# Norms in two halves of tokens, with the low parts made for two chunks at once

## The reference

```
# first block, per layer
h = layer_norm(ALPHA * h + 0.5 * swiglu(h, up1, down1), g0, b0)
h = layer_norm(ALPHA * h + mixer(h), g1, b1)          # mixer ends with  merged @ w_o
h = layer_norm(ALPHA * h + 0.5 * swiglu(h, up2, down2), g2, b2)
# behind it the 16 learned tokens are dropped; second block, per layer
x = x + token_mixing(rmsnorm(x, g_mix), ...)          # ends with  merged @ w_out
x = x + swiglu_2(rmsnorm(x, g_ffn), ...)              # layer 0: dense
x = x + moe_swiglu(rmsnorm(x, g_ffn), ...)            # layer 1: router, 8 experts, top 2
return rmsnorm(x, g_final)

layer_norm(x, g, b) = (x - mean(x)) * rsqrt(mean((x - mean(x))**2) + 1e-5) * g + b
rmsnorm(x, g)       = x * rsqrt(mean(x*x) + 1e-6) * g
```

## Time and profile before

| | us |
|---|---|
| three runs | 2657.14, 2655.45, 2654.16 |
| median | 2655.45 |
| span of the profiled execution | 2653.2 |
| PE busy | 2561.1 (97%) |
| DVE busy | 1943.4 (73%) |
| ACT busy | 1614.8 (61%) |
| POOL busy | 377.1 (14%) |

### The profile page before, as it was taken

One profiled execution on the slowest core, in us unless ns is written; L12 is line 12 of the kernel. 1 busy time (PEld: TensorE's weight loads), 2 busy tenths in 40 slices (PEclk: granted clock), 3 DMA queues, 4 the chain that ended last, 5 costly groups with the idle time before them and its releaser, 6 DMA issues.

```text
span 2653.2 us, 65470 instructions
## 1 busy us (share of the span) xinstructions
PE 2561.1 (97%) x27736; PEld 2159.7 (81%) x27736; DVE 1943.4 (73%) x1886; ACT 1614.8 (61%) x1690; POOL 377.1 (14%) x440
## 2 busy tenths in 40 slices
PE   9999999999999999999999999999999999999998
PEld 8887788888887888897888888799778687787775
DVE  5467675564567765666765466689999999999997
ACT  4346653354357654455654446657888888887876
POOL 3211322121105221103021103031000000000000
PEclk9999999999999999999999999999999999999999
DMA  8574355555555655554455655378999999999996
GB/s 268 172 210 141 108 195 197 169 190 188 157 161 152 199 182 181 177 192 132 148 197 192 190 190 163 118 273 340 412 419 422 419 413 422 413 418 418 413 421 273
DMA packets 345255, 666.16 MB, mean 251 GB/s; under 512 B 20448, under 2 KB 273536, under 8 KB 306096
## 3 DMA queue, kind: packets, MB, share of 16 engines
q1 hardware_dynamic: 344192, 661.39, 69.0%
q0 software_dynamic: 528, 0.63, 0.3%
q10 hardware_dynamic: 288, 0.59, 0.1%
HBM read 661.49 MB, written 1.05 MB: 250 GB/s over the span
## 4 chain that ended last, share of the span: by engine, by line
PE 62%; DVE 19%; DMA 7%; ACT 6%; issue 4%; DVEq 2%; POOLq 0%; ACTq 0%; POOL 0%; SPq 0%
PE ps L2336 17%; PE ps L2338 17%; PE ps L2337 17%; DVE w_lo L1621 7%; DMA w<-in_moe_units 3%; DVE work L1621 2%; DMA mix<-in_moe_units 2%; DVE ff L1621 2%; DVE w_lo L1461 2%; ACT w_hi L958 2%; ACT w_hi L849 2%; DMA squares_and_low<-in_moe_units 1%; PE ps L2379 1%; PE ps L2385 1%; PE ps L2380 1%
## 5 line engine op out<-in xcount | busy, mean ns | idle before, releaser
L2336 PE MATMUL ps<-x_hi,w_hi 128*128 128x96 f16 (+2 forms) x5024 | 1076.1, 246 | 19.1 <-DVE w_lo L1621 5.8
L2338 PE MATMUL ps<-x_hi,w_lo 128*128 128x96 f16 (+2 forms) x5024 | 1075.4, 246 | 7.3 <-issue 7.3
L2337 PE MATMUL ps<-squares_and_low,w_hi 128*128 128x96 f16 (+2 forms) x5024 | 1075.5, 246 | 4.3 <-issue 4.3
L1461 DVE SCALAR_TENSOR_TENSOR w_lo<-w,w_hi 128x2048 f16<-128x2048 f32 (+4 forms) x335 | 680.8, 2043 | 295.0 <-ACT w_hi L849 293.2
L849 ACT ACTIVATE w_hi<-w 128x2048 f16<-128x2048 f32 (+4 forms) x335 | 556.8, 1671 | 85.7 <-PE ps L2338 74.8
L2336 PEld LDWEIGHTS ps<-x_hi,w_hi 128*128 128x128 f16 x5024 | 492.6, 98 | 76.0 <-issue 15.9
L2337 PEld LDWEIGHTS ps<-squares_and_low,w_hi 128*128 128x128 f16 x5024 | 492.6, 98 | 50.0 <-issue 5.3
L2338 PEld LDWEIGHTS ps<-x_hi,w_lo 128*128 128x128 f16 x5024 | 492.4, 98 | 49.1 <-issue 7.4
L2338 PE MATMUL ps<-ff,w_lo 128*128 128x272 f16 (+1 forms) x880 | 243.3, 276 | 0.0
L2337 PE MATMUL ps<-ff,w_hi 128*128 128x272 f16 (+1 forms) x880 | 243.3, 276 | 0.0
L2336 PE MATMUL ps<-ff,w_hi 128*128 128x272 f16 (+1 forms) x880 | 243.3, 276 | 0.0
(11 more groups left out here) (408 smaller groups left out, 4770.9 us busy)
## 6 DMA issues: line engine op xcount, KB each, us to landing
w<-in_ffn_w_up_units SPq DMA_DIRECT2D x176, 512.0 KB, 4.6
w<-in_moe_units SPq DMA_DIRECT2D x75, 1024.0 KB, 11.9
w<-in_moe_units SPq DMA_DIRECT2D x56, 1280.0 KB, 15.3
mix<-in_moe_units SPq DMA_DIRECT2D x50, 1024.0 KB, 12.0
w<-in_w_in SPq DMA_DIRECT2D x96, 512.0 KB, 4.8
mix<-in_moe_units SPq DMA_DIRECT2D x36, 1280.0 KB, 15.6
w<-in_mix_w_in SPq DMA_DIRECT2D x60, 512.0 KB, 5.0
squares_and_low<-in_moe_units SPq DMA_DIRECT2D x26, 1024.0 KB, 12.0
```

Of the source, the lines that this page charges most:

```text
L1461: vec.scalar_tensor_tensor(k.w_lo[:, s, 0:size], k.w32[:, s, 0:size], WS, k.w_hi[:, s, 0:size], ALU.mult, ALU.subtract).then_inc(k.parts_r ...
L2336: pe.matmul(acc, w_hi, x_hi, start=first, stop=False)
L2337: pe.matmul(acc, w_hi, x_lo, start=False, stop=False)
L2338: return pe.matmul(acc, w_lo, x_hi, start=False, stop=last)
```

## The change

Each of the eight seams goes in two halves of tokens (2 x 136 or 2 x 128). The last two units of down, and the last of wo and of layer 0's wout, are gone through twice, once for each half, into two banks of their own; three tiles into the second half PE makes the sums of the first. DVE, ACT and the sums work half by half, and the opening of the next product takes all eight chunks of the first half, with the sums of the second half behind its fourth chunk, and then the second half. Low parts are used two chunks behind the high ones. The 13 fillers of a norm go.

On DVE, centring, scaling by the reciprocal and the low parts take two chunks in one instruction. Weight and bias columns are no longer in these: a new tensor_scalar with two columns writes the residual `h` for each chunk and half, from which the low part is taken. ACT makes the high part of each chunk and half with both columns (scale and bias), and no longer writes the residual. The splits of the next product's third unit move: DVE's from ahead of the last addition to behind the norm (or, behind wo, into the next product's own program), ACT's to between the second root and the second half's high parts. The second layer's router norm keeps its form.

The diff, cut to the programs' core (`th` is a half of the tokens, PAIRS is 4):

```diff
-KEEP_WARM = 13
...
+END_BANKS, MEAN_BANKS, VAR_BANKS, RMS_BANKS = (6, 7), (4, 7), (5, 6), (5, 4)
+OPEN_TOGETHER, LAG, SUMS_AT = 5, 2, 3
...
-    for u in range(phase.units):
+    for u in range(phase.units - 1):
...
+        def high(p, pair):
+            th = part_of(t, p)
+            act.wait_ge(k.ln_scaled, 2 * PAIRS * n + PAIRS * p + pair + 1)
+            for c in (2 * pair, 2 * pair + 1):
+                if last:
+                    act.activation(k.sq2[:, c, part_of(ALL2, p)], k.sq[:, c, th], ACT.Square, bias=column(k, b0 + c),
+                                   scale=column(k, g0 + c)).then_inc(k.rms_squared, 1)
+                else:
+                    act.activation(k.x_hi[:, c, th], k.sq[:, c, th], ACT.Identity, bias=column(k, b0 + c),
+                                   scale=column(k, g0 + c)).then_inc(k.x_hi_ready, 1)
...
+        squares_of_end(0)
+        rest_square(0)
+        root(0)
+        high(0, 0)
+        high(0, 1)
+        squares_of_end(1)
+        high(0, 2)
+        rest_square(1)
+        high(0, 3)
+        root(1)
         if following is not None:
             split(following + 2, q, UNIT)
...
+        def over_pair(x):
+            return x.unsqueeze(1).broadcast_to([P, 2, (t.stop - t.start) // 2])
+        def centered(p, pair):
+            th = part_of(t, p)
+            x = k.h[:, 2 * pair:2 * pair + 2, th]
+            vec.tensor_tensor(x, x, over_pair(k.ps[:, MEAN_BANKS[p], th]), ALU.subtract)
+        def inverse(p):
+            th = part_of(t, p)
+            vec.wait_ge(k.ln_std, 2 * n + p + 1)
+            vec.reciprocal(k.rstd[:, 0, th], k.std[:, 0, th])
+            vec.drain()
+        def normed(p, pair):
+            th, c = part_of(t, p), slice(2 * pair, 2 * pair + 2)
+            vec.tensor_tensor(k.sq[:, c, th], k.h[:, c, th], over_pair(k.rstd[:, 0, th]), ALU.mult).then_inc(k.ln_scaled, 1)
+            if pair + 1 < PAIRS:
+                centered(p, pair + 1)
+            vec.drain()
+            for c in (2 * pair, 2 * pair + 1):
+                vec.tensor_scalar(k.h[:, c, th], k.sq[:, c, th], column(k, g0 + c), column(k, b0 + c), ALU.mult, ALU.add)
+        def low(p, pair):
+            if n < LN_PARTS:
+                th, c = part_of(t, p), slice(2 * pair, 2 * pair + 2)
+                vec.wait_ge(k.x_hi_ready, high_before(n, False) + KC * p + 2 * pair + 2)
+                vec.tensor_tensor(k.x_lo[:, c, th], k.h[:, c, th], k.x_hi[:, c, th], ALU.subtract).then_inc(k.x_ready, 1)
         vec.drain()
-        def t(c):
-            vec.scalar_tensor_tensor(k.sq[:, c, cols], k.h[:, c, cols], column(k, g0 + c), k.rstd[:, 0, cols],
-                                     ALU.mult, ALU.mult).then_inc(k.ln_scaled, 1)
-            if c + 1 < KC:
-                u(c + 1)
-        def lo(c):
-            return vec.scalar_tensor_tensor(k.x_lo[:, c, cols], k.sq[:, c, cols], column(k, b0 + c), k.x_hi[:, c, cols], ALU.add, ALU.subtract)
-        def plain(c):
-            vec.tensor_scalar(k.h[:, c, META:T1], k.sq[:, c, META:T1], column(k, b0 + c), None, ALU.add)
-        for c in range(KC + 1):
-            if last:
-                if c < KC:
-                    t(c)
-                if c > 0:
-                    plain(c - 1)
-            else:
-                scaled(c, t, lo, (n + 1) * KC)
-            vec.drain()
+        add_end(0)
+        vec.drain()
+        spread(0)
+        centered(0, 0)
+        inverse(0)
+        normed(0, 0)
+        normed(0, 1)
+        low(0, 0)
+        add_end(1)
+        normed(0, 2)
+        low(0, 1)
+        spread(1)
+        normed(0, 3)
+        low(0, 2)
+        centered(1, 0)
+        inverse(1)
+        low(0, 3)
+        for pair in range(PAIRS):
+            normed(1, pair)
+            if pair:
+                low(1, pair - 1)
+        vec.drain()
+        low(1, PAIRS - 1)
+        if following is not None:
+            split(following + 2, q, UNIT)
...
+        add_end(0)
+        inverse(0)
+        normed(0, 0, 4)
+        low(0, 0)
+        add_end(1)
+        normed(0, 4, 6)
+        low(0, 1)
+        normed(0, 6, KC)
+        low(0, 2)
+        inverse(1)
+        low(0, 3)
+        for pair in range(PAIRS):
+            normed(1, 2 * pair, 2 * pair + 2)
+            if pair:
+                low(1, pair - 1)
+        low(1, PAIRS - 1)
+        if following is not None:
+            split(following + 2, 0, UNIT)
...
+        for p in range(2):
+            for kc in range(OPEN_TOGETHER if p else KC):
+                high(p, kc, range(2))
+                if kc >= LAG:
+                    low(p, kc - LAG, range(2))
+                if (p, kc) == (0, SUMS_AT) and second_sums is not None:
+                    second_sums()
+            if p == 0:
+                for kc in range(KC - LAG, KC):
+                    low(p, kc, range(2))
+        for j in range(2):
+            for kc in range(OPEN_TOGETHER, KC):
+                high(1, kc, [j])
+            for kc in range(OPEN_TOGETHER - LAG, KC):
+                a = low(1, kc, [j])
             a.then_inc(k.unit_done, 1)
...
+        g = phase.first + phase.units - 2
+        for p in range(2):
+            th = part_of(t, p)
+            for second in range(2):
+                if p == 0:
+                    weights(g + second, q)
+                    pe.wait_ge(k.ff_ready, gates + (2 + (1 + second) * half))
+                acc, tiles = k.ps[:, END_BANKS[p], 0:th.stop - th.start], [(c * P, P, second * half + c) for c in range(half)]
+                if (p, second) == (1, 0):
+                    chain(acc, g % SLOTS, tiles[:BEFORE_SUMS], a_hi[:, :, th], a_lo[:, :, th], last=False)
+                    first_sums()
+                    tiles = tiles[BEFORE_SUMS:]
+                a = chain(acc, (g + second) % SLOTS, tiles, a_hi[:, :, th], a_lo[:, :, th], first=(p, second) == (0, 0), last=bool(second))
+                if p == 1:
+                    a.then_inc(k.unit_done, 1)
+            if p == 0:
+                a.then_inc(k.first_half_out, 1)
...
+    def end_sums(n, p, first, evacuated):
+        th = part_of(kept(n), p)
+        if p == 1:
+            pe.wait_ge(k.vec_evac, evacuated)
+        pe.wait_ge(k.rest_summed, n + 1)
+        pe.matmul(k.ps[:, MEAN_BANKS[p], th], k.mean_w[:, :], k.prod[:, 1, th], start=True, stop=False)
+        pe.wait_ge(k.squares_summed, n + 1)
+        pe.matmul(k.ps[:, VAR_BANKS[p], th], k.mean_w[:, :], k.prod[:, 0, th], start=True, stop=False)
+        if first < KC - 1:
+            for c in (4, 5):
+                pe.wait_ge(k.ln_squared, squares_before(n) + c + 1)
+                pe.matmul(k.ps[:, VAR_BANKS[p], th], k.mean_w[:, :], k.sq[:, c, th], start=False, stop=False)
+        if p == 0:
+            pe.wait_ge(k.first_half_added, n + 1)
+        for c in range(first, KC):
+            a = pe.matmul(k.ps[:, MEAN_BANKS[p], th], k.mean_w[:, :], k.h[:, c, th], start=False, stop=c == KC - 1)
+        a.then_inc(k.ln_rest, 1)
+        pe.wait_ge(k.end_squared, 2 * n + p + 1)
+        for c in range(first, KC):
+            a = pe.matmul(k.ps[:, VAR_BANKS[p], th], k.mean_w[:, :], k.sq[:, c, th], start=False, stop=c == KC - 1)
+        a.then_inc(k.ln_var, 1)
```

More of the change, by code:

```diff
@@ L941, in residual @@
-    def residual(b0, t):
-        for c in range(KC):
-            a = act.activation(k.h[:, c, t], k.sq[:, c, t], ACT.Identity, bias=column(k, b0 + c))
-        a.then_inc(k.h_ready, 1)
+        for pair in range(PAIRS):
+            high(1, pair)
     def rms_square(c):
@@ L962, in wout_squares @@
         root_ready()
-        for c in range(KC):
+        for c in range(KC if l == DEPTH - 1 else 6):
             if l == DEPTH - 1 and c == 0:
@@ L2358, in all_out, with opening @@
         pe.wait_ge(k.act_evac, act)
-    def opening(phase, q, evac, evac0, x_hi, x_lo, t, chunk, n_step, kc_step, late=False, both=TOGETHER, first_banks=(0, 2)):
+    def opening(phase, q, evac, evac0, x_hi, x_lo, t, chunk, n_step, kc_step, banks=(0, 2)):
         weights(phase.first, q)
-        if not late:
-            weights(phase.first + 1, q)
-        banks, free = first_banks, 1 if late else 2
-        pe.wait_ge(evac, evac0 + (phase.base + free))
+        pe.wait_ge(evac, evac0 + (phase.base + 1))
         def tile(j, n, kc):
@@ L2573, in rms_norm @@
[L2573 to L2581 removed]
+        opening(phase, q, k.vec_evac, vec0, k.x_hi, k.x_lo, t, chunk, P, 256, (2, 0))
+        g = phase.first + 2
+        weights(g, q)
+        pe.wait_ge(k.vec_evac, vec0 + 2 + (phase.base + 1))
```

479 lines of the change are left out of this document (250 added, 229 removed).

## The result

The changed kernel took 2666.9 us (median of 5 runs, 2662.8 to 2669.5) against 2655.45: ratio 1.0044, interval 1.0032 to 1.0055. A second set of five runs, beside other runs of the kernel before, gave 2665.2 against 2655.63 (1.0034, interval 1.0021 to 1.0048). So it is some 10 to 11 us slower. The forecast was 2658.0, no measurable change; the range of 2648 to 2667 just reaches the time.

A forecast was written before the change was run, and what follows sets the result against it. PE is busy 97% of the span and only the eight seams before the router could pay, their lost time filled by DVE; 1.3 + 1.6 + 1.5 + 1.3 + 2.1 - 0.8 - 2.0 - 2.4 = +2.6 us gave 2658.0, range 2648 to 2667.

The forecast's parts named there:

- The bound of the LayerNorm seams: Stretches from a product's last two units over a LayerNorm to the next's third: DVE sets the end, first by 4.9 us.
- The pace of the half-width matmuls: On PE in the seams: matmuls of 136 columns start 0.059 us apart, those of 128 columns 0.056.
- the two-column form: DVE's new multiply-and-add with weight and bias columns, also writing the residual: 0.35 us, between 0.29 and 0.42.
- the walk of the first seam: First LayerNorm seam, DVE step by step: free at 190.26, low part ended 211.46, PE's third unit 1.3 us later.
- the signs of seams 1 to 6: LayerNorm seams: first five slower, +1.3, +1.6, +1.5, +1.3, +2.1 us; the sixth, last LayerNorm with first rms, faster, -0.8.
- the rival of slow half-width matmuls: All seams: half-width matmuls at 0.08 us let PE pass DVE; +33 us, about 2690; chance 0.03.
- The rival in which PE sets the LayerNorm seams: LayerNorm seams: DVE's pairs cost 4.9 us less a seam, so PE sets the ends; -23 us, 2632; chance 0.08.
- the granted clock at 1.00 in the seams: All seams: expected sign in the profile that PE keeps its full clock, 2.4 GHz, no stretch of half clock.
- the walk itself: Eighth seam, rms: PE waits for DVE's split, addition and square until 1535.7; third unit at 1550.3 against 1552.73, -2.4 us.
- a rival of 0.08: Seams: waits inside the halves without fillers may bring half clock; two such stretches +6 us, 2664; chance 0.08.
- "their sums take 1.27" behind wo: Second seam: after both last chunks are added at 365.23 the sums take 1.27 us; the seam comes to +1.6 us.
- the whole of the seventh seam: Rms seam behind wout: PE sets the end, 48 for 66 matmuls and two chunks to add; -2.0 us.

The follow-up runs named there:

- extra_op: Changed kernel with one more DVE tensor_tensor over two chunks, result unread, in each of the four steps of the second half; 2668.97 us.
- old_form: Changed kernel with the halves' arithmetic taken from the kernel before, the residual written by ACT again; 2659.11 us.
- after_again: The changed kernel unaltered, measured and profiled once more; 2665.2 us.
- fill6: Changed kernel with six small unread matmuls on PE ahead of the first half's sums in every seam; 2660.57 us.
- pool_free: Changed kernel with PE taking over POOL's last sums behind wo and wout; 2658.47 us.
- fill_pool: Changed kernel with its own arithmetic, four small PE matmuls ahead of the first half's sums, and PE taking over POOL's last sums; 2660.21 us.
- combo: Changed kernel with four small PE matmuls ahead of first-half sums, PE taking POOL's last sums, and the kernel before's arithmetic in the halves; 2654.14 us.

## Why the prediction was wrong

**Right.** The bound of the LayerNorm seams: DVE sets their ends, shown by extra_op (later by what it adds) and old_form (earlier by what it saves). The pace of the half-width matmuls (0.059 and 0.056), the two-column form (0.346 for 0.35), the walk of the first seam to 0.1 us, of the third to 0.1, and the signs of seams 1 to 6. The same starts refute the rival of slow half-width matmuls. (The Trainium skill's 81 ns for 128 columns, "TensorE: Matmul & The Clock Gate", section "Back-to-back issue gap", does not agree with this trace either, which has 56.) The rival in which PE sets the LayerNorm seams did not come true.

**Wrong, first step: "the granted clock at 1.00 in the seams".** In the eighth seam the walk itself contains the wait: PE stops at 1533.4 and goes on at 1535.7, 2.3 us. The clock fell behind it. The text had this as a rival of 0.08 and argued it away by comparing the new waits with 1.38 us and with fillers; but the new wait is longer than any that the kernel before has in a seam (1.66 us from start to start), and no fillers stand in it. The clock cost 1.0 us in the seventh seam and 1.6 in the eighth (after_again against fill6), less than half of the 6 that the rival was priced at; its chance was far too low. fill6 shows the cause.

**Wrong, second step: "their sums take 1.27" behind wo, and the whole of the seventh seam.** Both took PE's sums as ready once DVE and ACT were. PE's order puts POOL's sum first, and in each of these seams one of POOL's additions takes 2.6 us beside DVE's split where 0.73 to 0.76 is its time otherwise. That costs 0.8 us in seams 2 and 5 each (pool_free) and 0.8 in the seventh (fill_pool against fill6); with the clock's 1.0 the forecast of -2.0 became +0.3, of which 0.5 us stay without a cause that was shown. The forecast followed DVE, ACT and PE instruction by instruction and left POOL out. The price stood in the trace of the kernel before, 2.75 us at 364.16; there it did not show, since DVE's last addition came as late (366.88 to 367.32). pool_free shows the cause.

**Not foreseeable.** The late transfer in the profiled execution (2.9 us with the clock's part); in the fourth seam DVE stands still for 0.43 us with nothing to wait for ("issue" in the row at 765.95 of after_again), which is its +0.4. The pause belongs to the program: both profiles of the changed kernel, fill6, pool_free and fill_pool have it at the same instruction, extra_op in the third seam, old_form and combo in neither. Its cause stays open.

Corrected by the runs the sum of the seams is 1.3 + 2.6 + 1.5 + 1.7 + 2.9 - 1.1 + 0.3 - 0.6 = +8.6 us, 6.0 above the forecast: 2.6 by the clock, 2.4 by POOL, 0.4 by the pause, and some 0.6 of small errors. With the late transfer it is the 11.5 of the first measurement, if the transfer came late in most of its runs, which one profile can't show; some 1 us up to the 9.6 of the second lies outside the seams, and its cause stays open.
